# TensorE's two loops over the last three quarters of each MLP, written out as a straight program with constant waits

## What is computed

```python
def sq_relu_mlp(x, g, w_up, w_down):
    return jnp.square(jax.nn.relu(rmsnorm(x, g) @ w_up)) @ w_down
...
        hp = hp + sq_relu_mlp(hp, norm_mlp[layer], mlp_w_up[layer], mlp_w_down[layer])
        hs = hs + sq_relu_mlp(hs, norm_mlp[layer], mlp_w_up[layer], mlp_w_down[layer])
```

## Time and profile before

| | us |
|---|---|
| median of 3 executions | 2961.33 |
| lowest and highest | 2958.95, 2961.46 |
| span of the profiled execution (first to last instruction) | 2955.7 |
| PE busy in it | 2905.3 |
| DVE, ACT busy | 1441.9, 1057.9 |

### The profile page before, as it was taken

How to read it: one execution, slowest core, us unless ns; L and a number is a source line. 1 busy time by engine, 2 the same in 40 slices (tenths; PEclk the granted TensorE clock), 3 DMA queues, 4 the chain that set the end, 5 groups by cost and what they waited for, 6 DMA issues and landing times.

```text
span 2955.7 us, 45474 instructions
## 1 busy us (share of the span) xinstructions
PE 2905.3 (98%) x18745; PEld 2840.7 (96%) x18745; DVE 1441.9 (49%) x1483; ACT 1057.9 (36%) x1190; POOL 203.9 (7%) x108
## 2 busy tenths in 40 slices
PE   6999899999999999999999999999999999999999
PEld 6999769999999999999999999899999999999999
DVE  7568553643344344334365774446443443443443
ACT  3243432433233233233234642424433432332332
POOL 3100001200000000000120141112000000000000
PEclk9999989999999999999999999999999999999999
DMA  5423004444444444444444444334444444444443
GB/s 190 143 102 122 29 22 134 139 142 141 143 143 143 143 133 145 142 137 142 143 149 145 151 149 143 127 124 151 147 150 151 152 150 141 149 151 147 149 151 132
DMA packets 111355, 405.54 MB, mean 137 GB/s; under 512 B 12497, under 2 KB 13569, under 8 KB 111041
## 3 DMA queue, kind: packets, MB, share of 16 engines
q1 hardware_dynamic: 108000, 392.77, 39.8%
q0 software_dynamic: 1616, 6.35, 0.6%
q10 hardware_dynamic: 1552, 3.60, 0.3%
HBM read 396.58 MB, written 6.09 MB: 136 GB/s over the span
## 4 chain that ended last, share of the span: by engine, by line
PE 96%; DVE 3%; ACT 1%; issue 0%; DMA 0%; SPq 0%; DVEq 0%; ACTq 0%
PE PS L1235 30%; PE PS L1237 30%; PE PS L1236 30%; DVE xl L759 1%; PE PS L1328 1%; DVE w_lo L740 1%; PE PS L1364 1%; PE PS L1525 0%; PE PS L1526 0%; PE PS L1314 0%; PE PS L1502 0%; ACT pr L432 0%; DVE pr L810 0%; PE PS L1311 0%; PE PS L1653 0%
## 5 line engine op out<-in xcount | busy, mean ns | idle before, releaser
L740 DVE TENSOR_TENSOR w_lo<-stage,w_hi 128x1024 fp32r<-128x1024 f32 x742 | 934.2, 1261 | 1245.6 <-ACT w_hi L384 1245.2
L384 ACT ACTIVATE w_hi<-stage 128x1024 fp32r<-128x1024 f32 x742 | 785.6, 1059 | 1700.6 <-PE PS L1237 1692.8
L1235 PE MATMUL PS<-xh,w_hi 128*128 128x336 f32 (+1 forms) x3264 | 1035.3, 317 | 33.1 <-DVE w_lo L740 19.6
L1237 PE MATMUL PS<-xh,w_lo 128*128 128x336 f32 (+1 forms) x3264 | 1028.4, 315 | 0.0
L1236 PE MATMUL PS<-xl,w_hi 128*128 128x336 f32 (+1 forms) x3264 | 1026.5, 314 | 0.0
L1235 PEld LDWEIGHTS PS<-xh,w_hi 128*128 128x128 f32 x3264 | 616.0, 189 | 37.7 <-issue 20.4
L1235 PE MATMUL PS<-hh,w_hi 128*128 128x336 f32 (+1 forms) x2048 | 640.6, 313 | 0.0
L1237 PE MATMUL PS<-hh,w_lo 128*128 128x336 f32 (+1 forms) x2048 | 640.0, 312 | 0.0
L1236 PE MATMUL PS<-hl,w_hi 128*128 128x336 f32 (+1 forms) x2048 | 639.1, 312 | 0.0
L1236 PEld LDWEIGHTS PS<-xl,w_hi 128*128 128x128 f32 x3264 | 619.0, 190 | 1.2
L1237 PEld LDWEIGHTS PS<-xh,w_lo 128*128 128x128 f32 x3264 | 615.8, 189 | 0.0
(11 more groups left out here) (291 smaller groups left out, 1521.0 us busy)
## 6 DMA issues: line engine op xcount, KB each, us to landing
stage<-in_wstream SPq DMA_DIRECT2D x742, 512.0 KB, 3.3
out_y<-x ACTq DMA_DIRECT2D x4, 672.0 KB, 3.5
out_s<-so POOLq DMA_DIRECT2D x8, 256.0 KB, 2.6
x<-in_x_in SPq DMA_DIRECT2D x3, 672.0 KB, 9.7
dmask<-in_ret POOLq DMA_DIRECT2D x4, 360.0 KB, 4.9
s<-in_s_in POOLq DMA_DIRECT2D x1, 1024.0 KB, 5.1
x<-in_x_in SPq DMA_DIRECT2D x2, 336.0 KB, 4.5
tab<-in_tabs SPq DMA_DIRECT2D x1, 672.0 KB, 11.6
```

The lines of the kernel that those rows point to most:

```text
L384: act.activation(w_hi[:, s, :], stage[:, s, :], ACT.Copy).then_inc(hi_ready, 1)
L740: dve.tensor_tensor(w_lo[:, s, :], stage[:, s, :], w_hi[:, s, :].bitcast(F32), ALU.subtract).then_inc(lo_ready, 1)
L1235: pe.matmul(out, wh, rh, start=first, stop=False)
L1237: mm = pe.matmul(out, wl, rh, start=False, stop=last)
```

## The change

Both loops of PE are gone. A Python loop writes the same body four times, the first with the extras of quarter 0, and every wait then has a constant.

```diff
-            mlp(1, U_MLP0, G_MLP0, 0, True)(0)
-            with pe.Fori(1, 4) as f:
-                mlp(1, U_MLP0, G_MLP0, 0, False)(f)
+            for f in range(4):
+                mlp(1, U_MLP0, G_MLP0, 0, f == 0)(f)
...
-            mlp(3, U_MLP1, G_MLP1, 1, True)(0)
-            with pe.Fori(1, 4) as f:
-                mlp(3, U_MLP1, G_MLP1, 1, False)(f)
+            for f in range(4):
+                mlp(3, U_MLP1, G_MLP1, 1, f == 0)(f)
```

## The result

| | before | after |
|---|---|---|
| median, us | 2961.39 | 2944.93 |
| lowest to highest (4 executions each), us | 2958.95 to 2965.79 | 2943.74 to 2946.61 |
| span of the profiled execution, us | 2955.7 | 2941.7 |

The ratio of after to before is 0.9948, with a 95% interval of 0.9936 to 0.9961: 15.4 us, or 11.5 to 19 us. The forecast was 2948.7 us in a range of 2944 to 2957. A second measurement, among the experiments, gave 2945.58 us and a ratio of 0.9955 (0.9939 to 0.9972).

A forecast was written before the change was run, and what follows sets the result against it. PE, busy 2905.3 of 2955.7 us, was taken as the bound. Removing 12.6 us of jump surplus, other terms at zero, gave a 2943.1 us span, plus 5.6 us to the median: 2948.7 us, range 2944 to 2957.

The forecast's parts named there:

- The four jumps, 12.64 us: Jumps back after quarters 1 and 2 of both MLPs stop PE for code; removing them wins the 12.64 us surplus.
- The clock's part: Nearly all of 3.3 us of the surplus is the clock falling after two MLP gaps; counted as won too.
- Register work, entry and exit at nothing: PE's 378 register records of 32 ns before waits, and entering or leaving the loop, give nothing back.
- Longer code at nothing: Four repeated quarters become own code, 12 instruction packets each, priced at zero as in straight quarter 0.
- The slower rival: Fresh code arrives late, 48 packets at 0.95 us each, 45.6 us less 12.6 won: 2994.3 us; chance 0.06.
- No wait takes the gap's place: At quarter edges, constant waits on DVE's and ACT's work cause no new gap; `w_lo` is ready 8.2 us early.
- the profile named: Rival at the MLP edges: gaps are PE waiting for DVE's L792 and L740, nothing won, 2961.3 us; chance 0.06.
- four of the dearest jumps: Range's low end: all four MLP jumps like the dearest, surplus 4.34 us each, 17.4 us won, 2944.0 us.
- the 5.6 us between span and median: Whole kernel: the median lies 5.6 us above the profiled span, added to the forecast span of 2943.1 us.
- Cheap and dear jumps: MLP jumps in timed executions all cheapest, 4.2 us won, 2957.1 us, chance 0.08; or all dearest, 2944.0 us.

The follow-up runs named there:

- near and far jumps: Against the kernel before, MLP quarters 1 to 3 as short loops, twelve jumps of 3.1 packets: 2945.88 us; loop body of 9.3 packets: 2953.28 us.
- the kernel shifted by 64: The kernel before with 64 idle instructions added in quarter 0 of the first MLP, moving both loops: 2971.41 us, ratio 1.0044.
- the kernel shifted by 128: The kernel before with 128 idle instructions added in quarter 0 of the first MLP, moving both loops: 2951.6 us, ratio 0.997.

## Why the prediction was right, point by point

- **The four jumps, 12.64 us.** Right in sum and in each term, as the profile after has exactly the clean quarters. The mechanism (code beyond reach has to be brought in) was shown by the near and far jumps.
- **The clock's part.** Right: no fall inside an MLP in the changed kernel. That it comes after some long gaps and not after others was seen again. The premise, that without a gap a fall has no cause, is too wide: the one at 82.8 us of before came after PE had been without idle time for over 20 us. It holds for the MLPs of these profiles.
- **Register work, entry and exit at nothing.** Right: 360 ALU records in a kernel with no idle time.
- **Longer code at nothing.** Right: 147 packets in place of 159 and no gap inside a quarter. The slower rival was wrong about fresh code. Code that moves can cost something, though: 64 idle instructions made the kernel with loops 0.44% slower. A straight program has no far jump for such a shift to act on, but none was run shifted.
- **No wait takes the gap's place.** Right, and the releasers L792 and L740 that the profile named were false. It names them at gaps (start to start, less a step) of 1.7 us and more; at shorter ones it says "issue", and so it does at the second gaps of the kernel shifted by 64, of 2.7 to 3.0 us.
- **Base and size.** 2948.7 us against 2944.93. The time lies near the low end of the range, but not for the reason given for that end, four of the dearest jumps: the surplus was 12.6 and 13.9 us in the two profiles of before, not 17.4. The term that was mis-sized is the 5.6 us between span and median. Where an execution has both numbers the distance is 1.7 to 2.2 us (2943.74 and 2941.7 in after). So some 3.6 of the 5.6 us were no fixed distance but time within the kernel: the profiled execution of before was a quick one, about 2957.7 us, and the median one had that much more in it. By the same 2.0 us the forecast would have been 2945.1, and that this is within 0.2 us of the median is in part luck, as the executions of the changed kernel alone lie up to 2.9 us apart. It is likely that these microseconds are falls of the clock and dearer gaps, for the executions at 2966 to 2969 us have a mean granted clock of 0.988 to 0.990 and those at 2958 to 2960 us 0.991 to 0.993; where in the kernel they lie was seen for two executions only, neither of them a long one.
- **Cheap and dear jumps.** The range took the spread of gaps for the chance of an execution. It is mostly the place in a packet: about 1.1 to 1.8 us a gap at a good place, 2.3 to 3.0 at that of before (0.95 once in ten).

## What to carry to other kernels

A loop on PE is free while its body is short enough to be kept (6.2 packets, some 1590 instructions, was; 9.3 was not); beyond that each jump back stops PE for 1 to 3 us, and costs up to 5.8 us where the clock falls after it, and 5.8 to 6.8 us at the worst place seen (25.4 us for four). The end of what is kept was looked for only between these two lengths. Before writing a long loop out, look at the length of its jump records, at PE's timeline just behind them for a second gap, and at the count of instruction packets: here nearly the same time (ratio 0.9954) is had with 87 packets instead of 147 by nesting short loops. Where a kernel with far jumps changes by a few tenths of a per cent after an edit ahead of a loop, suspect the shift of its code first.

## What the runs showed that I had not expected

- Instructions that do nothing, ahead of a loop, moved the kernel from 2960.1 us to 2951.6 (128 of them) or 2971.4 (64), by their number alone.
- When two packets of instructions start together, the longer of them takes 2.0 to 2.6 us, in place of 0.9 to 1.4 for a lone one.
- A compare-and-branch is 0.07 to 0.09 us when not taken, 0.21 to 0.24 us when taken to code that is kept, and 3.3 to 5.2 us when not kept.
- The kernel before spreads wider than the changed one: 8 executions of the changed kernel lie within 2.9 us (2943.74 to 2946.61), 12 of the kernel before within 10.2 (2958.43 to 2968.65). Far jumps alone don't do it, as ten executions of the kernel shifted by 128, which has four, lie within 2.9 us too (2949.57 to 2952.45), and kernels without far jumps reached 2950.5.
